# Seven-product down chunks in a row, their hidden forms split at once, and one weight sum made by a load and an adding transfer

## The reference, cut to what matters

```python
def swiglu(h, w_gate, w_up, w_down):
    return (jax.nn.silu(h @ w_gate) * (h @ w_up)) @ w_down
# x = x + 0.5 * swiglu(rmsnorm(x, w), w_gate, w_up, w_down)     D_MODEL 1024, D_FF 2816, SEQ 256
```

## Time and profile before

| | us |
|---|---|
| median of 3 runs (1177.33 to 1177.52) | 1177.41 |
| span of the profiled execution | 1175.6 |
| PE busy | 1169.0 (99%) |
| DVE busy | 957.0 (81%) |
| ACT busy | 727.7 (62%) |
| POOL busy | 131.0 (11%) |
| DMA traffic | 230.71 MB, mean 196 GB/s |

### The profile page before, as it was taken

One profiled execution on the slowest core, in us unless ns is written; L12 is line 12 of the kernel. 1 busy time (PEld: TensorE's weight loads), 2 busy tenths in 40 slices (PEclk: granted clock), 3 DMA queues, 4 the chain that ended last, 5 costly groups with the idle time before them and its releaser, 6 DMA issues.

```text
span 1175.6 us, 17562 instructions
## 1 busy us (share of the span) xinstructions
PE 1169.0 (99%) x6769; PEld 1022.7 (87%) x6769; DVE 957.0 (81%) x1144; ACT 727.7 (62%) x967; POOL 131.0 (11%) x127
## 2 busy tenths in 40 slices
PE   9999999999999999999999999999999999999998
PEld 8888889889989888888888888889887898888886
DVE  6687898875657589889988979997886676797998
ACT  7566555854457566667565757564576566675773
POOL 1010001420142010100010001010012121100000
PEclk9999999999999999999999999999999999999999
DMA  9966755454445455979765779947623434678891
GB/s 322 332 207 199 200 194 179 145 179 144 144 143 180 144 181 173 270 218 268 226 202 166 229 217 263 269 145 213 209 89 135 135 118 156 208 225 251 245 258 69
DMA packets 168337, 230.71 MB, mean 196 GB/s; under 512 B 15312, under 2 KB 139600, under 8 KB 168144
## 3 DMA queue, kind: packets, MB, share of 16 engines
q1 hardware_dynamic: 163664, 213.30, 55.9%
q0 software_dynamic: 4464, 16.25, 7.3%
q10 hardware_dynamic: 144, 0.26, 0.1%
HBM read 213.02 MB, written 1.05 MB: 182 GB/s over the span
## 4 chain that ended last, share of the span: by engine, by line
PE 99%; POOL 0%; DVE 0%; issue 0%; POOLq 0%; DVEq 0%
PE ps L2334 30%; PE ps L2341 16%; PE ps L2313 15%; PE ps L2314 15%; PE ps L2315 15%; PE ps L2417 1%; PE ps L2611 1%; PE ps L3075 1%; PE ps L2931 1%; PE ps L3098 0%; PE ps L2619 0%; PE ps L3111 0%; PE ps L3036 0%; PE ps L3033 0%; PE ps L2485 0%; PE ps L2683 0%
## 5 line engine op out<-in xcount | busy, mean ns | idle before, releaser
L2334 PE MATMUL ps<-hT,w_parts 128*128 128x512 f32 x1568 | 374.9, 391 | 0.0
L2334 PEld LDWEIGHTS ps<-hT,w_parts 128*128 128x128 f32 x1568 | 290.0, 188 | 58.2 <-ACT w_parts L807 0.4
L1368 DVE TENSOR_TENSOR w_parts<-raw,w_parts 128x2048 fp32r<-128x2048 f32 x85 | 196.1, 2316 | 57.9 <-ACT w_parts L754 57.9
L2341 PEld LDWEIGHTS ps<-hT,w_parts 128*128 128x128 f32 x1568 | 201.4, 191 | 8.0 <-DVE w_parts L1444 0.2
L754 ACT ACTIVATE w_parts<-raw 128x2048 fp32r<-128x2048 f32 x85 | 162.3, 1920 | 72.8 <-PE ps L2315 69.8
L889 ACT ACTIVATE w_parts<-raw 128x2048 fp32r<-128x2048 f32 x108 | 206.0, 1907 | 0.6 <-DMA raw<-in_ffn_w_gate 0.6
L2341 PE MATMUL ps<-hT,w_parts 128*128 128x256 f32 x1568 | 204.1, 283 | 0.0
L1616 DVE TENSOR_TENSOR w_parts<-raw,w_parts 128x2048 fp32r<-128x2048 f32 x63 | 143.9, 2284 | 1.2 <-ACT w_parts L889 1.2
L2313 PE MATMUL ps<-w_parts,arena_r 128*128 128x512 f32 (+1 forms) x234 | 91.2, 390 | 0.0
L2314 PE MATMUL ps<-w_parts,arena_r 128*128 128x512 f32 (+1 forms) x234 | 91.1, 389 | 0.0
L2313 PE MATMUL ps<-w_parts,hT 128*128 128x512 f32 (+1 forms) x240 | 91.0, 379 | 0.0
(11 more groups left out here) (375 smaller groups left out, 2123.5 us busy)
## 6 DMA issues: line engine op xcount, KB each, us to landing
raw<-in_ffn_w_down SPq DMA_DIRECT2D x44, 1024.0 KB, 5.0
raw<-in_ffn_w_gate SPq DMA_DIRECT2D x43, 1024.0 KB, 5.4
raw<-in_ffn_w_up SPq DMA_DIRECT2D x43, 1024.0 KB, 5.4
raw<-in_xattn_wkv SPq DMA_DIRECT2D x16, 1024.0 KB, 5.3
xn<-arena POOLq DMA_DIRECT2D x30, 512.0 KB, 5.6
raw<-in_even_w_in SPq DMA_DIRECT2D x13, 1024.0 KB, 5.1
raw<-in_xattn_wq SPq DMA_DIRECT2D x8, 1024.0 KB, 5.1
raw<-in_xattn_wo SPq DMA_DIRECT2D x8, 1024.0 KB, 5.3
```

What stands on the lines that cost most here:

```text
L1368: ins = V.tensor_tensor(lo, src, hi.bitcast(F32), ALU.subtract)
L2334: mm(ps[:, bank0 + m, :], cols(w_hi, n, k, CW, m * P, (m + 1) * P), hT[:, k, :, :].rearrange("p a c -> p (a c)"), start=k == 0, stop=False)
L2341: last = mm(ps[:, bank0 + m, SEQ:], cols(w_lo, n, k, CW, m * P, (m + 1) * P), hT[:, k, 0, :], start=False, stop=k == KT - 1)
```

## The change

Mixed turns become 4 to 8 in f = 0 and 1 to 8 in f = 1 to 3, on every engine in one loop: 5 + 3 x 8 = 29. The scheme of the seven products is rewritten so that the hidden values and their sums lie side by side (`gu_forms`, seven blocks of 128x128): one ACT instruction makes all the high parts (128x896) and one of DVE the low parts. The number of gu_sum instructions goes from four to three (the first is 256 wide), that of w_sums on DVE from four to three. The fourth sum is made by transfers: SP loads one 128x512 block of the down chunk again, straight into `Mixed.w_sums[:, 0, :]`, and POOL issues a transfer that reads another block from memory and adds it there. ACT's high part of the sums waits for that transfer (`row_added`). The order on DVE and ACT in the turn changes, `down_split` frees the down slot for SP ahead of `lo_done`, and f = 0 adds its kept sums by transfer as the others do. The core of the diff:

```diff
         class Mixed:
-            FIRST, COUNT = (2, 0, 0, 0), (3, 7, 7, 7)
+            TURN, COUNT = (4, 1, 1, 1), (5, 8, 8, 8)
...
@@ SP: turn(j, after_mixed, with_row) @@
+                        if c == 2 and after_mixed:
+                            sp.wait_ge(down_split, j + (down_split_at(f, 0) + 1 - behind))
                         sp.dma_start(slot_k(n, width), ...)
+                        if c == 2 and with_row:
+                            sp.wait_ge(lo_done, j * 3 + (base + 2))
+                            sp.dma_start(Mixed.w_sums[:, 0, :],
+                                         w[bass.ds(j, 1), :, 1, 0:512].rearrange("a p c -> (a p) c"))\
+                              .then_inc(row_in, 16)
...
@@ ACT: turn @@
                     up_out(j, j * 3 + (base + 1))
+                    if out is not None:
+                        act.wait_ge(mixed_mm, out + (mixed_mm_at(f, 0) + 1))
+                        copied(0)
                     split(base + 3 + RING)
...
-                    if mixed is not None:
-                        act.wait_ge(gu_summed[f], gu_sums_at(f, mixed) + 4)
-                        nc.scalar.activation(Mixed.gu_hi, Mixed.gu_sums, ACT.Copy)
-                    hidden(j + (f * FJ + 1), gu_hi)
+                    if mixed is None:
+                        hidden(j + (f * FJ + 1), gu_hi)
+                    else:
+                        forms(mixed)
+                    if out is not None:
+                        copied(1)
...
+                        act.wait_ge(w_summed, mixed * 3 + (w_sums_at(f, 0) + 1))
+                        nc.scalar.activation(w_hi[:, m, :], raw[:, m, :], ACT.Copy).then_inc(hi_done, 1)
+                        act.wait_ge(row_added, mixed * 16 + (row_added_at(f, 0) + 16))
+                        act.wait_ge(w_summed, mixed * 3 + (w_sums_at(f, 0) + 3))
+                        nc.scalar.activation(Mixed.w_hi, Mixed.w_sums, ACT.Copy).then_inc(w_sums_hi, 1)
...
@@ DVE: turn_mixed (turn_mixed_next is gone) @@
                     gate_sum(j)
                     gate_scale(j)
                     split(base + 2 + RING)
                     up_sum(j)
                     product(j)
+                    gu_sum(i, 0, gu_forms[:, 0:3:2, :], gu_forms[:, 2:5:2, :], gu_forms[:, 1:3, :], ALU.subtract)
+                    gu_sum(i, 1, gu_forms[:, 5, :], gu_forms[:, 2, :], gu_forms[:, 1, :], ALU.add)
+                    gu_sum(i, 2, gu_forms[:, 6, :], gu_forms[:, 3, :], gu_forms[:, 5, :], ALU.subtract)
+                    dve.wait_ge(raw_in[m], (j - 1) * 16 + landed(n))
+                    w_sum(i, 0, slot[:, 0, :], slot[:, 1, :], slot[:, 0, :], ALU.subtract)
                     split(base + 3 + RING)
+                    w_sum(i, 1, Mixed.w_sums[:, 1, :], slot[:, 2, :], slot[:, 0, :], ALU.subtract)
+                    forms_low(j)
+                    w_sum(i, 2, Mixed.w_sums[:, 2, :], slot[:, 3, :], Mixed.w_sums[:, 1, :], ALU.subtract)
+                    dve.wait_ge(hi_done, (j - 1) * 3 + (n + 1))
+                    V.tensor_tensor(w_lo[:, m, :], raw[:, m, :], ..., ALU.subtract).then_inc(down_split, 1)
+                    dve.wait_ge(w_sums_hi, i + (w_sums_hi_at(f, 0) + 1))
+                    V.tensor_tensor(Mixed.w_lo, Mixed.w_sums, ..., ALU.subtract).then_inc(lo_done, 1)
...
@@ POOL: ffn @@
+                for i in range(Mixed.COUNT[f]):
+                    pool.wait_ge(row_in, row_at(f, i) + 16)
+                    pool.dma_start(Mixed.w_sums[:, 0, :], down_blocks(f)[Mixed.TURN[f] + i, :, 0, 0:512],
+                                   accum_op=ALU.add).then_inc(row_added, 16)
+                    for half in range(2 if i > 1 else 0):
...
...
@@ PE: mixed_down @@
-                for bank, a, ai, b, bi in ((0, g, 0, w, 0), (1, g, 1, w, 1), (4, g, 2, w, 2), (5, gu_sums, 2, w, 3),
-                                           (6, g, 3, w_sums, 2), (2, gu_sums, 1, w_sums, 1), (3, gu_sums, 0, w_sums, 0)):
+                for bank, a, ai, b, bi in ((0, g, 1, w, 1), (1, g, 2, w, 0), (5, g, 3, w, 3), (4, g, 6, w, 2),
+                                           (7, g, 4, w_sums, 2), (2, g, 5, w_sums, 1), (3, g, 0, w_sums, 0)):
```

More of the change, by code:

```diff
@@ L427, in build @@
         g_act = part(0, [512])
-        gu = part(512, [512])
-        gate_lo, gate, up_lo, up = (part(1024 + 512 * i, [2, SEQ]) for i in range(4))
+        gu_forms = part(512, [7, P])
+        gu = part(512 + P, [512])
+        gate_lo, gate, up_lo, up = (part(1408 + 512 * i, [2, SEQ]) for i in range(4))
         squares_out = part(3072, [TT, 2, 512])
@@ L714, in ffn @@
                                 sp.dma_start(dst, src).then_inc(small_in, 16)
-                with sp.Fori(8 if first else 0, FJ - 1) as j:
-                    turn(j)
+                    turn(8, True, True)
+                    turn(9, True)
+                else:
+                    turn(0)
+                    turn(1, False, True)
+                    with sp.Fori(2, FJ - 2) as j:
+                        turn(j, True, True)
+                    turn(9, True)
                 n = base + FFN_CHUNKS - 1
@@ L895, in turn, with copied @@
                     up_out(j, j * 3 + (base + 1))
+                    def copied(half):
+                        if added:
+                            if f or not isinstance(out, int) or out > 1:
+                                act.wait_ge(kept_added_in[half], out * 16 + kept_added_at(f, 0))
+                        nc.scalar.activation((Mixed.copied if added else Mixed.kept)[half], ps[:, 2 * half:2 * half + 2, :],
+                                             ACT.Copy).then_inc(mixed_read, 1)
@@ L904, in turn @@
-                    if out is not None:
[L905 to L910, removed]
@@ L955, in ffn @@
                     turn(4, lambda c: c and squares(1, mem_rows, lambda t, h: act.wait_ge(mem_in, 16), tiles=(c - 1,)),
[L956 to L961, removed]
+                         mixed=0)
                 else:
                     turn(1, mixed=0)
[L964 to L970, removed]
+                first = Mixed.TURN[f]
+                turn(first + 1, mixed=1, out=0)
+                turn(first + 2, mixed=2, out=1, added=True)
+                with act.Fori(3, Mixed.COUNT[f]) as i:
+                    turn(i + first, mixed=i, out=i - 1, added=True)
+                if f == 0:
+                    turn(FJ - 2, small_tables)
+                else:
+                    turn(FJ - 2)
                 made[0] = base + FFN_CHUNKS - 1
@@ L1644, in turn_read @@
+                    V.tensor_tensor(Mixed.w_lo, Mixed.w_sums, Mixed.w_hi.bitcast(F32), ALU.subtract).then_inc(lo_done, 1)
                 def turn_read(j, i):
@@ L2404, in mixed_down @@
                     if bank == 1:
[L2405 removed]
+                        last.then_inc(mixed_mm, 1)
                 return last
```

251 lines of the change are left out of this document (96 added, 155 removed).

## The result

The changed kernel takes 1188.96 us (median of 4 runs, 1187.8 to 1190.41) against 1177.44 before: ratio 1.0098, 95% interval 1.0086 to 1.0111. It is slower by 1%, where a gain of 0.3% was forecast. The rival of transfers that fall behind had been priced at 1186 with a chance of 0.20, and the range ended at 1181.

The account below looks back on a forecast made before the run. PE, busy 1169.0 of 1175.6 us, was taken as the bound. Its matmuls saved 3.4 us and transfers were costed at nothing, so the median 1177.41 less 3.4 gave 1174.0 us, with a range from 1173.3 to 1181.

Parts of the forecast that it names:

- The rival of transfers that fall behind: Mixed turns with kept sums: late row sum or transfers over 15.89 us make PE wait at `lo_done`; 1186 us, chance 0.20.
- What PE is spared: PE in mixed turns: 3 matmuls of 0.227 us fewer in each of five more turns, 3.4 us saved.
- DVE's and ACT's side: DVE's mixed turn falls from 15.88 to 15.0 us, and the new ACT and DVE order still meets PE in time.
- The row of DVE's turn before: DVE's mixed turn before the change, 469.93 to 485.81, 15.88 us, was read as having no idle time.
- The move of the first copy ahead of the up split: On ACT, copying banks 0 and 1 before the up split costs nothing as long as transfers are on time.
- The row sum as a chain: Row load, row add, high and low part in a mixed turn: middle value 10 to 12 us, limit 12.8, so covered.
- The transfers as a whole: DMA work of a turn with kept sums: 15.4 to 16.9 us against 15.89; excess 0.4 a turn, costed at nothing.
- the crowded turn: Window 492.67:509.25 before the change gave 2.8 us per MB of load, so a new turn asks for 16.6 us.
- the 3.2 us: Slack in a mixed turn: DVE's last low part ends at 500.5, PE wants the whole chunk at 503.8.
- the loads' 4: Slack of a down load that lands after 5.0 us: some 4 us more before DVE waits.
- The rule of the Trainium skill: For DMA transfers, 2.0 us plus bytes at 436 GB/s: row add 2.6 us, a turn's DMA work 10.8, none late.

Follow-up runs that it names:

- Experiments 1: Changed kernel with the fourth weight sum made on DVE again and no row load or row adding transfer: 1174.72 us, ratio 0.9976.
- experiment 3: Changed kernel without POOL's transfers that add the kept sums and without their waits, leaving out part of the down product: 1174.4 us, ratio 0.9973.
- 9: Changed kernel with rows sent to spare memory, the fourth sum left out and no ACT wait for the row: 1188.47 us, ratio 1.0082.
- experiment 8: Changed kernel with POOL's add of the kept sums' first half issued ahead of the wait for the row load: 1207.3 us, ratio 1.025.
- experiment 4: Changed kernel with the first stage's small strided loads moved to turns 2 and 3: 1185.35 us, ratio 1.0062.
- experiment 7: Changed kernel with strided loads moved to turns 2 and 3 and five mixed turns in every stage: 1183.3 us, ratio 1.0048.
- experiments 6: Changed kernel with the fourth sum on DVE and only the row's adding transfer, into spare memory, one row load per stage: 1182.48 us, ratio 1.0034.
- 2: Changed kernel with the fourth sum on DVE and both row transfers sent to spare memory, their data not waited for: 1194.66 us, ratio 1.0139.
- load-only kernel: Changed kernel with the fourth sum on DVE and only the row load, into spare memory, no row add: 1175.02 us, ratio 0.9987.

## Why the prediction was wrong

- **What PE is spared** was right: 15 matmuls, 3.4 us. Experiments 1 and 3 give back 2.9 and 3.2 us of it.
- **DVE's and ACT's side** was right: DVE's turn has room (14.3 to 14.8 us busy in the windows where PE kept its pace), and with DVE's sum put back the schedule still holds at 15.5 busy. The row of DVE's turn before was not quite without idle time, as the prediction has it; the timeline shows 0.19 us. The move of the first copy ahead of the up split costs nothing.
- **The row sum as a chain** was right as far as it went: the add lands after 4.0 to 7.6 us, and the wait for it costs nothing that can be told (experiments 3 and 9). The chain, put at 10 to 12 us in the middle, takes 12.2 to 12.9 in crowded turns, because the row load lands after up to 10.0 us, where at most 7.5 had been allowed. That its limit is near was shown by experiment 8.
- **The transfers as a whole: this is the step that failed.** It gave 15.4 to 16.9 us of DMA work for a new turn, 16.6 by the crowded turn, "an excess of 0.4 us a turn adds up to 2.4 in six turns", and "I therefore cost it at nothing". Measured, the DMA engines' turn is 16.6 us, so the excess is 0.7, and the slack that was to take it in is less than the 3.2 us and the loads' 4. Both are taken apart below.
- **What I had not costed at all** is the first stage: the strided loads stood in the diff and the trace, on SP's queue right behind the row loads of turns 6 and 7, and I said nothing of them. They are 3.6 us of the 14 by the medians of experiment 4, a quarter. By the trace the stage loses 4.8 us, 1.2 of it by the lower clock behind the stall, which the prediction did not have either.
- **The rule of the Trainium skill** (DMA: Bandwidth & Descriptors, "Anatomy of one DMA"), 2.0 us plus the bytes at 436 GB/s, gave by an estimate 10.8 us of DMA work in a turn and no loss. The runs contradict it for adding transfers: it gives 2.6 us for the 256 KB of a row's add, and the 29 of them landed after 4.0 to 7.6.
- **The rival** had the mechanism right: the transfers need more than a turn, and PE waits in `mixed_down` for DVE, whose gate_sum stands right behind the last low part. That its 1186 lies near 1189 is luck. It needed 17.1 us a turn and put 12 us in three stages; at the measured 16.6 its own sum gives about 1177. The last three stages lost 8.7 us, 3 a stage, and the first stage's 4.8 were not in it. What was off was its chance, and a slack that made 16.6 look harmless.

**The size of the excess.** That the crowded turn gave 16.6 too is in part chance, for the prediction's 16.6 is packet time, from which the overlap of the queues still had to be taken (16.6 / 1.04 = 16.0). What was too low is the price of the adding transfers when the queues are full. The queues in the crowded turn of before, then in 528.23:544.12 of the changed kernel (packets, MB, share):

```profile
q1 hardware_dynamic: 2875, 3.67, 63.2%
q0 software_dynamic: 288, 1.05, 32.9%
...
q1 hardware_dynamic: 2371, 3.24, 58.1%
q0 software_dynamic: 432, 1.31, 47.1%
```

Loads took 2.9 us per MB in both. Adding transfers took 5.2 in the first, 5.4 in the prediction's sum and 5.7 in the second. A new turn has 3.41 MB of the one and 1.31 of the other, 17.2 us of packet time. The mean share over the four turns shown is 1.03, which makes it 16.7 us.

**The slack.** I counted the slack of a single transfer. By the prediction's own sum 16.6 us a turn costs 4.3 less 3.2, 1.1 us a stage; the last three stages lost 2.6, 1.8 and 4.3. So they took in about 1.7, 2.5 and none of the 4.3. With a backlog each load of the ring is late and hands its delay on, and in the last turn of a stage DVE also reads the kept sums; how much each of the two takes from the slack is argued and not measured. Three turns of excess already cost something (experiment 7).

How the slack of a stage's end divides between the last reads of the kept sums and the loads of the next stage was not tried, and why f = 3 has the least of it stays open. Both row transfers together without POOL's wait for the row load were not tried either, so the 12 us between experiments 6 and 2 are not divided between the load's packets and the place of the kept sums behind it. Nor was the spread of the load-only kernel explained, which runs at 1174.6 to 1175.1 in most executions and at up to 1179.2.

## What to carry to other kernels

Before work is moved from an engine with no room to the DMA engines, add up the packet time of a turn there as one would for an engine, at rates from a stretch where the queues are full, and compare it with the turn: here, at 0.96, there was room for one plain 256 KB load, with nothing to spare, and not for an adding transfer. An excess in a ring of buffers does not show in the first turns, and it is not forgiven for being small: it is summed over the turns in a row. And look at everything that stands behind a new transfer in its queue, small strided loads too.

## What the runs showed of the hardware

- An adding transfer costs the DMA engines twice what a plain one of its size does: 5.4 us per MB inside the chip's own memory, 1.49 us for 256 KB from outside (5.7 per MB), where plain loads take 2.6 to 3.1. When both queues are full it is 5.7 per MB for the two kinds together (47.1% of 15.89 us for 1.31 MB).
- Two plain loads of 8 KB in small pieces held SP's queue for 6.7 us beside the adding transfers of kept sums, and for 4.37 us in the trace of before and 3.66 in that of experiment 3, where none of these run.
- Behind two waits of 0.80 and 1.76 us in one turn PE's granted clock fell: 0.93 in the mean of the next turn, the same kind of matmul 0.63 us and not 0.40, and 17.13 us for the work of 15.89.
- The place in POOL's queue decides: behind an adding transfer of 512 KB that of 256 KB landed after 8.4 us, and after 4.2 when it was issued first.
- 0.6 us of work a turn on DVE, hidden when all is on time, is worth 6 us in 29 turns once the transfers are late (1194.66 against 1188.47).
